# The MLP of a decoder block: three quarters of its width in twelve groups over all tokens, up products by Strassen's scheme, and two other orders

## The reference: what is computed

```python
h = rmsnorm(x, norm_pre_mlp[l])
ff = jnp.square(jax.nn.relu(h @ mlp_w1[l])) @ mlp_w2[l]
x = x + rmsnorm(ff, norm_post_mlp[l])
```

## Time and profile before

| | |
|---|---|
| time, median of 3 runs | 2458.06 us (2457.84 to 2458.24) |
| the profiled execution | 2457.88 us, its span 2455.9 us |
| PE busy | 2423.9 us, 99% of the span |
| DVE / ACT / POOL busy | 1547.8 / 672.5 / 1325.1 us (63% / 27% / 54%) |
| chain that ended last | PE 93%, DVE 4%, all others 1% or less |
| HBM read, written | 226.18 MB, 46.14 MB; 111 GB/s over the span |
| the MLP | from about 1739 us to the end |

### The profile page before, as it was taken

The page is one execution under the profiler, slowest core; times in us unless marked ns, Lnnn a source line. Parts: engine busy times, 40 slices in busy tenths (PEclk is TensorE's granted clock), DMA queues, the critical chain, the costliest instruction groups (busy, mean ns, idle before and its releaser), DMA issues.

```text
span 2455.9 us, 32326 instructions
## 1 busy us (share of the span) xinstructions
PE 2423.9 (99%) x11950; PEld 1997.1 (81%) x11950; DVE 1547.8 (63%) x1715; ACT 672.5 (27%) x961; POOL 1325.1 (54%) x1028
## 2 busy tenths in 40 slices
PE   8999999999999999999999999999999999999997
PEld 5788888888788888887888888888888888888887
DVE  6789888888878888877865629453851231522123
ACT  4443442554122222221023124253421010211001
POOL 0777773333222222234667767736766666666664
PEclk9999999999999999999999999999999999999999
...
GB/s 278 113 88 109 129 112 120 60 68 52 77 44 43 43 43 51 64 99 159 249 184 141 149 129 182 178 61 120 162 95 94 95 102 95 163 94 96 101 94 120
DMA packets 86855, 273.54 MB, mean 111 GB/s; under 512 B 8048, under 2 KB 11376, under 8 KB 85744
## 3 DMA queue, kind: packets, MB, share of 16 engines
...
HBM read 226.18 MB, written 46.14 MB: 111 GB/s over the span
## 4 chain that ended last, share of the span: by engine, by line
PE 93%; DVE 4%; issue 1%; ACT 1%; DMA 1%; POOL 0%; ACTq 0%; SPq 0%; DVEq 0%; POOLq 0%
PE ps L450 28%; PE ps L452 28%; PE ps L451 28%; PE xb L651 1%; PE ps L504 1%; PE xb L680 1%; PE xb L683 1%; PE xa L671 1%; DVE h_lo L931 1%; PE xb L452 0%; PE xb L450 0%; PE xb L451 0%; DVE xb L943 0%; DVE x_sb L935 0%; PE xb L658 0%
## 5 line engine op out<-in xcount | busy, mean ns | idle before, releaser
L2343 POOL TENSOR_TENSOR w_lo<-w_raw,w_hi 128x1024 fp32r<-128x1024 f32 x278 | 703.6, 2531 | 23.2
L2340 POOL TENSOR_TENSOR small<-small 128x1 f32<-128x1 f32 x278 | 74.2, 267 | 966.3 <-PE ps L452 785.1
L450 PE MATMUL ps<-yb_hi,w_hi 128*128 128x512 f32 x1024 | 402.0, 393 | 4.2 <-POOL w_lo L2343 3.1
L452 PE MATMUL ps<-yb_hi,w_lo 128*128 128x512 f32 x1024 | 399.2, 390 | 0.0
L451 PE MATMUL ps<-yb_lo,w_hi 128*128 128x512 f32 x1024 | 399.1, 390 | 0.0
L450 PE MATMUL ps<-h_hi,w_hi 128*128 128x512 f32 x928 | 369.0, 398 | 0.2 <-DVE hg_zc L1344 0.2
L452 PE MATMUL ps<-h_hi,w_lo 128*128 128x512 f32 x928 | 362.5, 391 | 0.0
L451 PE MATMUL ps<-h_lo,w_hi 128*128 128x512 f32 x928 | 362.2, 390 | 0.0
L2341 POOL TENSOR_SCALAR w_hi<-w_raw 128x1024 fp32r<-128x1024 f32 x278 | 309.1, 1112 | 0.0
L450 PE MATMUL ps<-hx_hi,w_hi 128*128 128x512 f32 x736 | 288.3, 392 | 0.0
L452 PE MATMUL ps<-hx_hi,w_lo 128*128 128x512 f32 x736 | 286.3, 389 | 0.0
...
## 6 DMA issues: line engine op xcount, KB each, us to landing
w_raw<-wall SPq DMA_DIRECT2D x298, 512.0 KB, 3.6
gst<-gate_d SPq DMA_DIRECT2D x24, 512.0 KB, 4.9
w_kv<-wall SPq DMA_DIRECT2D x16, 512.0 KB, 4.9
x_d<-xx ACTq DMA_DIRECT2D x16, 512.0 KB, 3.4
raw_odd<-wall SPq DMA_DIRECT2D x14, 512.0 KB, 4.3
xs_xa<-x_d ACTq DMA_DIRECT2D x12, 512.0 KB, 5.8
...
```

The source lines that it names most:

```text
L450: nc.tensor.matmul(out, wh, xh, start=start, stop=False, skip_group_check=onto)
L452: return nc.tensor.matmul(out, wl, xh, start=False, stop=stop, skip_group_check=onto)
L2340: nc.gpsimd.tensor_tensor(small[:, 13:14], small[:, 12:13], small[:, 12:13], ALU.add)
L2343: nc.gpsimd.tensor_tensor(w_lo[:, u], w_raw[:, u], w_hi[:, u].bitcast(F32), ALU.subtract).then_inc(w_split, 1)
```

## The change

**Order of the MLP.** The first half of the tokens goes through up block 0 and down block 0 as before. Blocks 1 to 3, three quarters of the width, are then cut into twelve groups of 256 channels. Each group works over all 1024 tokens: seven products of 12 matmuls for the up side (Strassen's scheme as in the earlier stage), and for the down side 2 x 4 products of 12 matmuls, `down_group(g, 1)` for the second token half and then `down_group(g, 0)`. Then follow up block 0 and down block 0 of the second half (`up_last`, `last_block`). The down products of a group sum over 256 channels only and are added into `xx` in SBUF by DVE, 1024 columns at a time (`down_sum`). PSUM banks `xa` and `xb` take them in turn; the last group uses other banks for its last four.

**Weights of a group.** Fifteen ring slots of 128x512: seven for the up side (four sums of quarters by POOL, three quarters as loaded), eight loaded for the down side (256 KB each). Seven buffers, `MLP_RING`. ACT makes all high parts (`ring_high`), POOL all low parts (`ring_low`). SP loads the two 512 KB up tiles of the next group behind the first down slot of this one.

**Activations.** The groups need x of both halves normalised alike, so `token_ratio` on DVE scales the second half by the ratio of the two norm factors and the gain (8 instructions), `token_sums` makes the four sums (6 instructions of 128x2048), and `token_lows` five low parts of 128x2048; ACT makes five high parts of that size, one of them by the name `yb_hi`. `chain(3, ...)` no longer makes the high and low parts of the second half. Before up block 0 of the second half, four of its eight tiles have to be brought back from HBM (`xe_d`, `bx`) and split (`last_split`).

**Two other orders.** At the start of the earlier Strassen stage ACT does the sigmoid `sigb` before the copy of `t4`. Before the branch products SP issues the first weight tile ahead of two branch loads and the second one behind them.

The diff, cut to what the prediction speaks of:

```diff
+GROUPS = (FFB - 1) * KB // 2
+PER = 7 + KB
+SLOTS = GROUPS * PER
...
+MLP_RING = (5, 6, 4, 2, 3, 0, 1)
+AHEAD = len(MLP_RING)
...
+            def up_product(g, i, out, moving, start):
+
+                n = PER * g + i
+                slot = ring_slot(n)
+                pe.wait_ge(s_split, BLOCK_OLD + n + 1)
+                for j in range(KB // 2):
+                    hi, lo = moving(j)
+                    mm = mm3(out, m_hi[slot][:, j], m_lo[slot][:, j], hi, lo, start and j == 0, j == KB // 2 - 1, not start)
+                mm.then_inc(seven_done, 1)
+
+            def up_group(g):
+
+                x = group_x(g)
+                pe.wait_ge(evac[0], N_B // 2 - 1)
+                pe.wait_ge(up_relued, 4 * g)
+                up_product(g, 0, x, x_pieces(0, 0), True)
+                pe.wait_ge(evac[1], N_B // 2)
+                pe.wait_ge(t_split, 4 + 1)
+                up_product(g, 1, z_bank, t_sums(0), True)
+                pe.wait_ge(part_copied, PART_OLD + 3 * g + 1)
+                pe.wait_ge(t_split, 4 + 2)
+                up_product(g, 2, x, t_sums(1), False)
+                pe.wait_ge(part_copied, PART_OLD + 3 * g + 2)
+                pe.wait_ge(t_split, 4 + 3)
+                up_product(g, 3, z_bank, x_pieces(1, 1), False)
+                pe.wait_ge(part_copied, PART_OLD + 3 * g + 3)
+                pe.wait_ge(t_split, 4 + 4)
+                up_product(g, 4, x, t_sums(2), False)
+                up_product(g, 5, y_bank, x_pieces(1, 0), True)
+                pe.wait_ge(part_added, PART_OLD + 3 * g + 2)
+                pe.wait_ge(t_split, 4 + 5)
+                up_product(g, 6, x, t_sums(3), False)
...
+            def down_group(g, h):
+
+                pe.wait_ge(h_split, KB + 4 * g + (2 if h else 4))
+                for d in range(KB // 2):
+                    n = down_slot(g, h, d)
+                    before = KB * g + (1 - h) * KB // 2 + d - 1
+                    slot = ring_slot(n)
+                    pe.wait_ge(s_split, BLOCK_OLD + n + 1)
+                    if before > 0:
+                        pe.wait_ge(xacc_done, KB + before)
+                    for o in range(2):
+                        for k in range(2):
+                            hi, lo = ff_piece(2 * h + k)
+                            mm = mm3(down_banks(g, h, d)[:, o * HALF:(o + 1) * HALF], m_hi[slot][:, 2 * o + k],
+                                     m_lo[slot][:, 2 * o + k], hi, lo, k == 0, k == 1)
+                    mm.then_inc(seven_done, 1)
+
+
+            for g in range(GROUPS):
+                up_group(g)
+                down_group(g, 1)
+                down_group(g, 0)
...
+            pe.wait_ge(t_split, 9 + 1)
+            pe.wait_ge(xacc_done, KB + KB * GROUPS - 1)
+            for j in range(4):
+                up_last(j)
+            pe.wait_ge(ff_split, 2 * KB)
+            last_block(N_B + KB)
...
                 pair(0)
-                pre_low(c, 0)
+                if c < 3:
+                    pre_low(c, 0)
...
+            def token_ratio():
+
+                ratio = nacc[0][:]
+                done(v.reciprocal(ratio, rn[0][:]))
+                root(3, 4)
+                done(mul(ratio, ratio, rn[1][:]))
+                dve.wait_ge(x_stored, 16 * 16)
+                dve.wait_ge(xnsq_done, 16)
+                for odd in range(2):
+                    for t in range(odd, KB, 2):
+                        scaled(xx[1][:, t], xx[1][:, t], par[:, t, G_PRE_MLP:G_PRE_MLP + 1], ratio).then_inc(h_normed, 1)
+
+            def token_sums():
...
+                dve.wait_ge(h_normed, KB + KB // 2)
+                done(sub(t1, x12, x11[0]))
+                sub(t1, t1, x11[1]).then_inc(t_summed, 1)
+                dve.wait_ge(h_normed, KB + KB)
+                dve.wait_ge(t_summed, 4 + 1)
+                sub(t2, x22, t1).then_inc(t_summed, 1)
+                dve.wait_ge(t_summed, 4 + 2)
+                done(sub(t4, x21[0], t2))
+                add(t4, t4, x21[1]).then_inc(t_summed, 1)
+                sub(t3, x22, x12).then_inc(t_summed, 1)
+
...
+            def group(g):
+
+                x = group_x(g)
+                parts = [p[:] for p in m_part]
+                up_sum(g, 0, parts[2], z_bank)
+                up_sum(g, 1, parts[1], x)
+                piece_low(g, 0, 2, parts[2])
+                up_sum(g, 2, parts[0], y_bank)
+                piece_low(g, 1, 3, parts[1])
+                dve.wait_ge(seven_done, BLOCK_OLD + PER * g + 7)
+                dve.wait_ge(h_split, KB + 4 * g + 1)
+                up_relu_group(parts[2], x)
+                piece_low(g, 2, 0, parts[0])
+                down_sum(g, 1, 0)
+                piece_low(g, 3, 1, parts[2])
+                for d in range(1, 4):
+                    down_sum(g, 1, d)
+                if g < GROUPS - 1:
+                    for d in range(4):
+                        down_sum(g, 0, d)
+                    return
+                last_split()
+                for d in range(4):
+                    down_sum(g, 0, d)
+                    if d == 2:
+                        v.tensor_copy(rn[1][:], rn[0][:])
+                    for t in (2 * d - 1, 2 * d):
+                        last_sum(0, t)
+
+            chain(3, lambda j: plain_up(N_MLP // 2, 0, j))
+            up_low(0, 3)
+            token_ratio()
+            token_sums()
...
 
             block_high(0)
-            act.wait_ge(t_summed, 4)
-            copy(t4[:, 0::2, HALF:], t4_sum[:, 0::2, 0:HALF]).then_inc(t_hi_done, 1)
-            block_high(1)
             act.wait_ge(keys_stored, 32)
             act.wait_ge(kv_stored, 32)
             act.wait_ge(mm_done, N_CONF + 1)
             a.activation(sigb[:], ps[0][:], ACT.Sigmoid).then_inc(evac[0], 1)
+            act.wait_ge(t_summed, 4)
+            copy(t4[:, 0::2, HALF:], t4_sum[:, 0::2, 0:HALF]).then_inc(t_hi_done, 1)
+            block_high(1)
...
+            def ring_high(n):
+
+                if n >= SLOTS:
+                    return
+                g, h, i = slot_role(n)
+                slot = ring_slot(n)
+                full = m_raw[slot][:]
+                if h is not None:
...
+            def group(g):
+
+                n, x = PER * g, group_x(g)
+                for i, bank in enumerate((x, z_bank, x)):
+                    keep_up(g, i, bank)
+                    ring_high(n + 4 + i)
+                ring_high(n + 7)
+                for i, (piece, part) in enumerate(((2, 2), (3, 1), (0, 0), (1, 2))):
+                    piece_high(g, i, piece, part)
+                    if i < 3:
+                        ring_high(n + 8 + i)
+                for i in range(11, PER + 4):
+                    ring_high(n + i)
+
+
+            chain(3, lambda j: up_square(N_MLP // 2 + j, 0, j))
+            act.wait_ge(x_stored, 16 * 16)
+            down_copies(0)
+            norm_root(3, 4)
+            down_copies(1)
+            act.wait_ge(h_normed, KB + KB // 2)
+            act.dma_start(xe_d.rearrange("t p n -> p t n"), xx[1][:, 0::2]).then_inc(kv_stored, 16)
+            token_high(0)
+            down_copies(2)
+            token_high(1)
+            act.wait_ge(h_normed, KB + KB)
+            copy(yb_hi[1][:, 1::2], xx[1][:, 1::2]).then_inc(t_hi_done, 1)
+            down_copies(3)
+            act.wait_ge(mm_done, N_B)
+            token_high(2)
+            token_high(3)
+            for n in range(4):
+                ring_high(n)
+            for g in range(GROUPS):
+                group(g)
...
+            act.wait_ge(seven_done, BLOCK_OLD + PER * (GROUPS - 1) + 7)
+            act.wait_ge(kv_stored, 32 + 16)
+            act.dma_start(bx[:], xe_d.rearrange("t p n -> p t n")).then_inc(x_in[0], 16)
+            for j in range(4):
+                load_residual(4, j)
+            act.wait_ge(x_in[0], 16 + 16)
...
+            def ring_low(n, full):
+
+                slot = ring_slot(n)
+                pool.wait_ge(s_high, BLOCK_OLD + n + 1)
+                nc.gpsimd.tensor_tensor(m_lo[slot][:], full, m_hi[slot][:].bitcast(F32), ALU.subtract).then_inc(s_split, 1)
...
+            for g in range(GROUPS):
+                up_blocks(g)
+                for n in range(PER * g + 7, PER * g + PER):
+                    pool.wait_ge(down_loaded[ring_slot(n)], DOWN_OLD[ring_slot(n)] + 16 * (loads_before(n) + 1))
+                    ring_low(n, m_raw[ring_slot(n)][:])
+            for u in range(2):
+                split(last, u, BLOCK_OLD + (SLOTS - 5 if u == 0 else SLOTS), seven_done)
...
                 if g == 3:
+                    weights(m + 1, 0)
                     load_branch(2)
                     load_branch(3)
+                    weights(m + 1, 1)
...
+            def down_weights(n):
+
+                g, _, d = slot_role(n)
+                slot = ring_slot(n)
+                sp.wait_ge(seven_done, BLOCK_OLD + n + 1 - AHEAD)
+                rows = wall[bass.ds(W_GROUPS + 4 * g + 2 + d // 2, 1), :, d % 2 * HALF:(d % 2 + 1) * HALF]
```

(10 more changed lines are left out.)

355 lines of the change are left out of this document (232 added, 123 removed).

## The result

The changed kernel takes 2474.93 us (median of 4 runs, 2471.83 to 2478.44), the kernel before in the same job 2457.95: ratio 1.0067, 95% interval 1.0054 to 1.008. The forecast was 2474. The profiled execution took 2476.1 us, 2474.3 of them span, 18.4 more than the span before.

What follows compares the result with a forecast made beforehand. The prediction took PE, busy for 99% of the span, as the bound. 144 fewer matmuls (-32.6 us) and the added delays summed to +16.0 us, giving 2474 us; its own range was 2464 to 2486, the wider one 2457 to 2488.

Steps and rivals of the forecast that it cites:

- b: Before down block 0: PE waits for the chain behind the last hidden tiles; +6.6 us, bounds 4.5 and 9.
- h: Sigmoid first, Strassen stage: product 1 waits for the bank DVE frees with `gbuf`; +1.1 us, bounds -0.6 and 1.5.
- f: Before the last block: the chain behind the last hidden tiles, without DVE work between; +6.0 us, bounds 5 and 8.
- c: Down block 0: POOL's splits of weight tiles 6 and 7 late beside DVE's token sums; +10.1 us, bounds 0 and 14.
- d: First group's first product: waits for ACT's queued copies and POOL's low part; +10.1 us, bounds 8 and 12.
- e: Inside the twelve groups: the second hidden piece's low part comes late, 1.1 us a group; +13.2 us, bounds 0 and 25.
- The loads are the wait: Rival: the down slot behind two up tiles lands 1 us later than estimated, +14.4 us, 2488; chance 0.11.
- g: Last group: bank `ps0` is reused while its sum is queued behind `last_split`; +1.5 us, bounds 0 and 5.
- i: Weight order on SP before the branch stage: no effect, 0 us, bounds -1 and 1.
- DVE and POOL do not meet: Rival: wide DVE instructions leave POOL alone because the splits fall between them, 2447.5 us; chance 0.12.
- The groups run clean: Rival: the groups lose 0 to 0.3 us each and only the seams cost, 2461 us; chance 0.13.
- It simply pays: Rival: only the saving from 144 fewer matmuls is left, 2425.3 us; chance 0.04.

Runs made afterwards that it cites:

- e10_all_sums4: e9_all with DVE's first three wide token sums cut into four instructions of 128x512 each: 2446.12 us.
- e2_first: The changed kernel with the first ring slot's high copy on ACT ahead of down block 0's last copies, the next three ahead of the last two wide copies: 2472.93 us.
- e4_late: The changed kernel with the first weight tile of down block 0 and of the last block started when six of eight hidden tiles are split: 2465.96 us.
- e1_ring: The changed kernel with ACT's high copy of each group's second down slot put behind the second hidden piece's square and high copy: 2461.23 us.
- e5_loads: The changed kernel with each group's second down slot loaded on SP ahead of the next group's two up tiles: 2469.91 us.
- e9_all: The changed kernel with the edits of e1_ring, e4_late and e7_split_late, the sigmoid's old ACT order, and the first slot's high copy earlier: 2445.77 us.
- e7_split_late: The changed kernel with the last group's wide low part on DVE (`last_split`) moved behind the second down sum: 2470.21 us.

## Why the prediction was right, term by term

- *What bounds.* Right: every matmul removed paid its 0.2267 us, and every wait of PE was paid in full. The waits stood where the forecast put them in all seven terms from b to h.
- *b and f.* Right in mechanism. The gap is 5.14 us at both places, where 5.5 (b) and 4.3 (f) were taken: at f POOL's `w_lo` (2409.13 us) meets DVE's two low parts (from 2409.65, 2.98 us in place of 1.3) as it does at b, which the forecast left out for f. That is 0.8 of the 1.4 us by which f came out above its forecast; the rest is the clock, 2.2 us for the 1.7 charged.
- *c, the step that failed.* "The split for tile 6 ... is 3.3 us late; that for tile 7 ... 3.4 us late again after a tile at the slow clock": the waits were 1.7 and 2.0 us. The step that fails is "three instructions lengthened by 2.0 us": the middle one of the three, `w_hi`, took its 1.05 us in both splits, and it was DVE's sum beside it that waited (3.17 and 3.16 us for 2.29). So the splits took 6.8 and 7.6 us, not 9.6 to 10.5. And the clock fell behind one gap, not two. The forecast of c was 4.5 us too high.
- *d.* Right in sum: gap 7.2 for 8.4, clock 2.0 for 1.7. "So nothing more" was wrong: the second slot came 1.2 us late, because a POOL sum still beside the low parts took 3.3 us. e10_all_sums4 shows that c and d are not two terms but one, and e2_first and e4_late agree: DVE's token work and POOL's steps wait for each other, and PE is handed the delay at one seam or the other.
- *e.* The load's half was right and carried most of it: slot behind two up tiles, ACT's queue behind the slot, low part behind ACT. The slot landed 17.6 us into the group shown (17.3 taken), the low part was done at 20.5 (19.8 taken); 0.38 us of that is the meeting of DVE and POOL (1.06 for 0.68). e1_ring turned ACT's order and left 0.8 us of 15.6; e5_loads, which moved the load alone, left 8.4, in meetings. "The loads are the wait" (2488) named the right mechanism and the wrong size. The Trainium skill's rule (SBUF — State Buffer, "SBUF: two separate sides") agrees on the size of a meeting: 1.1 us at most, less than a POOL step of 1.3. With ACT's order turned eleven groups lose 0.8 (e1_ring) to 4.8 us (e9_all), where the forecast had worked out nearer 5 by the rule; with the load alone moved they lose 8.4 (e5_loads), between that and 13, because nearly every group has a meeting that costs almost a whole step. What made e 16 was the load, on which the rule has nothing to say.
- *g.* Mechanism right (e7_split_late), 3.0 for 1.5: the load of `bx`, issued at 2343.2, let the copy begin only at 2351.2, 8 us for the 7 taken.
- *h.* Right: PE waits for `gbuf` at product 1. +1.9 in the profiled pair, +1.5 over the fourteen traces, for 1.1.
- *i.* Open. *The clock.* Charging 1.7 us above 3 us and nothing below was too sharp a line: c's gap of 2.0 us had 1.8 us of slow clock behind it, see below.
- *The other rivals.* "DVE and POOL do not meet": POOL's `w_lo` beside the token sums took 4.3 us for 2.4, its sum beside the low parts 3.3 for 1.3. "The groups run clean" came true only with e1_ring's order: 2461.2 us, as it said. "It simply pays": the Trainium skill's advice (Perfetto Trace Analysis, "Identifying Performance Opportunities") to work on the most-contended engine names what a is worth, 32.6 us; the trace does not bear it out as a forecast, since b to g took 49.6 back, in waits for engines that were 32 to 68% busy.

The errors of c (-4.5) and of e, f and g (+2.8, +1.4, +1.5) offset each other: the sum was off by 2.2 us of the span, while the errors of the nine terms without their signs make 12.6. That the forecast of 2474 met the median within 1 us is luck in good part.
